# Mamba, attention, convolution and HGRN blocks on one core: shorter norm chains, attention's DVE and ACT steps on two blocks at a time, shuffled rotary partners

## The reference, cut to what matters

```python
# first two mixers:  h = rmsnorm(x, pre);  x = x + rmsnorm(mixer(h), post)
# the mamba mixer ends with:  y = rmsnorm(y, gate_norm);  return y @ w_out
def rmsnorm(x, w):
    return x * rsqrt(mean(x * x) + 1e-6) * w

# attention: 16 query heads, 4 key/value heads of 64, window 128, 4 blocks of 128 tokens
q, k = apply_partial_rope(q, cos, sin), apply_partial_rope(k, cos, sin)
# of each head's 64 rows, t1 = rows 0..7 and t2 = rows 8..15:
#   t1*cos - t2*sin,  t2*cos + t1*sin,  the rest as it is
s = (q . k) / 8, masked to the last 128 keys (256 key columns a block)
m = max(max(s), sink);  p = exp(s - m);  denom = sum(p) + exp(sink - m)
o = (p / denom) . v * silu(gate);  return o @ w_out
```

## Time and profile before

| what | us |
|---|---|
| three runs | 1970.71, 1975.97, 3117.33 (median 1975.97) |
| the profiled execution | 1969.06 |
| its span, first to last instruction | 1967.3 |
| PE busy / PEld busy in the span | 1872.2 / 1481.6 |
| DVE / ACT / POOL busy | 1078.4 / 611.2 / 905.7 |
| mean granted TensorE clock | 0.98 of full |

### The profile page before, as it was taken

How to read it: one execution, slowest core, us unless ns; L and a number is a source line. 1 busy time by engine, 2 the same in 40 slices (tenths; PEclk the granted TensorE clock), 3 DMA queues, 4 the chain that set the end, 5 groups by cost and what they waited for, 6 DMA issues and landing times.

```text
span 1967.3 us, 24972 instructions
## 1 busy us (share of the span) xinstructions
PE 1872.2 (95%) x9602; PEld 1481.6 (75%) x9602; DVE 1078.4 (55%) x1704; ACT 611.2 (31%) x1083; POOL 905.7 (46%) x910
## 2 busy tenths in 40 slices
PE   7999999897899897899999999999999999999997
PEld 5788877686676675558888888887777788888886
DVE  6888878834777756345333322148778753333212
ACT  5444445513333335023111100025566531111001
POOL 4444343354532245315555555554332455555552
PEclk9999999898999998999999999999999999999999
DMA  8676766576554454947889888896653498888884
GB/s 217 148 155 153 154 147 152 118 160 140 119 112 102 91 120 111 225 102 173 188 197 191 195 190 182 196 208 141 135 134 83 104 205 195 194 192 194 184 187 109
DMA packets 212838, 309.98 MB, mean 158 GB/s; under 512 B 22480, under 2 KB 166768, under 8 KB 212720
## 3 DMA queue, kind: packets, MB, share of 16 engines
q0 software_dynamic: 42624, 148.65, 44.2%
q1 hardware_dynamic: 165680, 154.34, 25.2%
q10 hardware_dynamic: 4416, 5.39, 1.1%
HBM read 153.18 MB, written 2.10 MB: 79 GB/s over the span
## 4 chain that ended last, share of the span: by engine, by line
PE 56%; DVE 1%; ACT 1%; ACTq 1%; DMA 1%; issue 1%; POOL 1%; DVEq 0%; POOLq 0%
PE gp L694 16%; PE gp L695 15%; PE gp L696 15%; PE mp L949 2%; PE mp L1025 1%; ACTq L1385 1%; PE gp L666 1%; PE gp L668 1%; PE gp L667 1%; PE gp L639 1%; PE gp L640 1%; PE gp L641 1%; PE mp L1075 0%; PE mp L1066 0%; POOL sqsum L564 0%
## 5 line engine op out<-in xcount | busy, mean ns | idle before, releaser
L584 POOL TENSOR_SCALAR wh<-stage 128x1024 fp32r<-128x1024 f32 (+2 forms) x298 | 344.1, 1155 | 906.0 <-PE gp L696 751.4
L694 PE MATMUL gp<-hh,wh 128*128 128x512 f32 x1512 | 607.4, 402 | 10.3 <-DVE m_raw L1661 4.3
L695 PE MATMUL gp<-hh,wl 128*128 128x512 f32 x1512 | 590.5, 391 | 0.0
L696 PE MATMUL gp<-hl,wh 128*128 128x512 f32 x1480 | 579.2, 391 | 0.0
L590 POOL TENSOR_SCALAR wl<-stage 128x1024 fp32r<-128x1024 f32 (+2 forms) x296 | 347.5, 1174 | 0.0
L694 PEld LDWEIGHTS gp<-hh,wh 128*128 128x128 f32 x1512 | 285.4, 189 | 77.3 <-issue 14.5
L695 PEld LDWEIGHTS gp<-hh,wl 128*128 128x128 f32 x1512 | 285.5, 189 | 58.5 <-issue 1.7
L696 PEld LDWEIGHTS gp<-hl,wh 128*128 128x128 f32 x1480 | 278.9, 188 | 59.9
L593 POOL DMA_DIRECT2D wl<-stage x296 | 261.9, 885 | 94.1 <-POOL wl L590 83.7
L2106 DVE TENSOR_TENSOR val<-gp,rstd 128x512 f32<-128x512 f32 x44 | 30.4, 691 | 203.9 <-PE gp L696 203.9
L694 PE MATMUL gp<-f_h,wh 128*128 128x512 f32 x352 | 137.2, 390 | 0.0
(11 more groups left out here) (352 smaller groups left out, 2805.7 us busy)
## 6 DMA issues: line engine op xcount, KB each, us to landing
wl<-stage POOLq DMA_DIRECT2D x263, 512.0 KB, 5.3
stage<-ffn_w SPq DMA_DIRECT2D x120, 512.0 KB, 4.2
stage<-ssm_w_in SPq DMA_DIRECT2D x32, 512.0 KB, 5.0
stage<-hg_w_in SPq DMA_DIRECT2D x32, 512.0 KB, 4.7
stage<-ssm_w_in SPq DMA_DIRECT2D x32, 256.0 KB, 5.0
stage<-ssm_w_out SPq DMA_DIRECT2D x16, 512.0 KB, 3.6
stage<-att_w_in SPq DMA_DIRECT2D x16, 512.0 KB, 4.7
stage<-cp_w_in SPq DMA_DIRECT2D x12, 512.0 KB, 5.4
```

The costliest lines, as they stand in the source:

```text
L584: pool.tensor_scalar(wh[:, s, part], stage[:, s, part], 1.0, 1.0, ALU.mult, ALU.mult).then_inc(hi_done, 1)
L694: pe.matmul(bank[:, :], wvh[:, cols], hi(kk), start=start, stop=False)
L695: pe.matmul(bank[:, :], wvl[:, cols], hi(kk), start=False, stop=False)
L696: mm = pe.matmul(bank[:, :], wvh[:, cols], lo(kk), start=False, stop=stop)
```

## The change

1. **Norm chains.** In both post-norms ACT squares the product straight out of PSUM, before DVE moves it to `yo` (a plain copy now). The gate norm's factor isn't applied: its epsilon is added to the sum of squares (`geps`), and Ln and Exp for `rg` go. In the two post-norms and the pre-norms of `att` and `cp` (`direct`) the eighth square isn't added; PE sums it by a second matmul. The table for Ln is loaded ahead of the last square.
2. **Pre-norms 0 to 2.** `val` goes; DVE forms the low part in one step, `xT*w - hh`. POOL's additions of squares go to DVE, between the residual steps. The sum stands in PE's program ahead of tile 7 of the lead units (`sum_early`).
3. **Tables** are made during `ssm_out`, after its fourth tile, with one more step (the sign of sin); ACT's Sin runs ahead of the last square.
4. **Rope.** The rotation matmuls go. DVE shuffles partner rows inside 32 partitions, then cos, sin and sum: four steps for three, at slots 4, 6 and 8. `turn_v` and `copy_v` have a semaphore of their own.
5. **Two blocks at a time.** `mask_scores`, `exps` and `normalise` handle two blocks of one head pair; the small steps are on 128x4. PE scores a pair in every second slot, ahead of `turn_p` and `pv`.
6. **Order.** A group's first slot has one granule and its second two (before: two and one). Setup of `kd`, the convolution's pads and `eye` moves ahead of the wait for `rstd`. `cp` runs 19 granules ahead of convolution 0 and 3 ahead of convolution 1 (before: 16 and 4).

```diff
     pre_round, post_round = [0, 2, 4, 5, 6, 7, 8], [1, 3]
+    direct = (1, 2, 3, 4)
+    own_eps = post_round[0]
...
-                for v, name in ((1, "att"), (2, "cp")):
-                    if u == phases[name][0] + 1:
-                        for k in range(1, KT):
-                            add_square(pool, pre_round[v], k)
...
             def sum_squares(r):
-                pe.wait_ge(sq_added, (KT - 1) * (r + 1))
-                pe.matmul(mp[3][:, :], ones[:, :], sqsum[:, :], start=True, stop=True).then_inc(sum_ready, 1)
+                pe.wait_ge(sq_added, adds_before(r + 1))
+                mm = pe.matmul(mp[3][:, :], ones[:, :], sqsum[:, :], start=True, stop=r not in direct)
+                if r in direct:
+                    pe.wait_ge(sq_ready, KT * (r + 1))
+                    mm = pe.matmul(mp[3][:, :], ones[:, :], sq[:, (KT - 1) % 2, :], start=False, stop=True)
+                mm.then_inc(sum_ready, 1)
...
                         if h < KVH:
                             late = h == KVH - 1
                             run(gran, ((1, 1, 1, 1, 1, 1, 1, 1, 0, 0, 0) if late else
-                                       (2, 1, 1, 1, 1, 1, 1, 1, 0, 1, 0))[k])
+                                       (1, 2, 1, 1, 1, 1, 1, 1, 0, 1, 0))[k])
...
                         if h:
+                            if k < 8 and k % 2 == 0:
+                                scores(h - 1, k // 2)
                             if 0 <= k - 2 < 8:
                                 turn_p(h - 1, k - 2)
                             if 0 <= k - 3 < 8:
                                 pv(h - 1, k - 3)
-                            if k < 8:
-                                scores(h - 1, k)
-                        if h < KVH and k == 9:
-                            rotate(h, (0, 1))
                     if h < KVH:
-                        rotate(h, (2,))
+                        turn_v(h)
...
-                run(gran, 16)
+                run(gran, 19)
                 convolve(0)
-                run(gran, 4)
+                run(gran, 3)
...
     # DVE, post_norm_of
+                    if k > 2:
+                        add_square(dve, pre_round[v], k - 2)
+                    if k:
+                        low_of_x(v, k - 1)
...
     # DVE, rope(h, j)
+                    shuffled = step(dve.stream_shuffle(rtmp[rows, 0, :], src, PARTNER))
+                    step(dve.tensor_tensor(rtmp[rows, 1, :], src, cosT[rows, :], ALU.mult))
+                    after(shuffled)
+                    step(dve.tensor_tensor(rtmp[rows, 0, :], rtmp[rows, 0, :], sinT[rows, :], ALU.mult))
+                    after()
+                    step(dve.tensor_tensor(dst, rtmp[rows, 0, :], rtmp[rows, 1, :], ALU.add))
...
     # DVE, the loop of attention
                         if h:
+                            if k == 6:
+                                gate_o(h - 1, 0)
                             if k == 11:
                                 gate_o(h - 1, 1)
-                            if 1 <= k <= 8:
-                                normalise(h - 1, k - 1)
-                            if k < 8:
-                                mask_scores(h - 1, k)
-                            if k == 6:
-                                gate_o(h - 1, 0)
+                            if k < 8 and k % 2:
+                                normalise(h - 1, k // 2)
+                            if k < 8 and k % 2 == 0:
+                                mask_scores(h - 1, k // 2)
...
-                            rope(h, (0, 1))
+                        if h < KVH and k in (4, 6, 8):
+                            rope(h, k // 2 - 2)
```

More of the change, by code:

```diff
@@ L238, in build, with adds_before @@
         n += count
+    unvalued = [split0[f"pre{v}"] for v in range(3)]
+    value0 = {name: n - KT * sum(u < n for u in unvalued) for name, n in split0.items()}
     y_split = [range(0, 4), range(4, 8), range(8, 10), range(10, 12), range(12, 13), range(13, 14)]
     pre_round, post_round = [0, 2, 4, 5, 6, 7, 8], [1, 3]
+    direct = (1, 2, 3, 4)
+    own_eps = post_round[0]
+    def adds_before(r):
+        return sum(KT - 1 - (i in direct) + (i == own_eps) for i in range(r))
     with ExitStack() as ctx:
@@ L618, in weights_at, with granules @@
                 return wh[:, s, at:at + un.cols], wl[:, s, at:at + un.cols]
-            def granules(name, hi, lo, split, lead=0, after_first=None, ahead=None):
+            def granules(name, hi, lo, split, lead=0, after_first=None, ahead=None, sum_early=False):
                 u0, u1, t0, _ = phases[name]
@@ L851, in mamba, with turn_v @@
                 run(gran_out)
-                pe.wait_ge(gate_rstd, 1)
+                pe.wait_ge(gate_eps, 1)
                 sum_squares(post_round[0])
             def attention():
[L856 to L870, removed]
+                gran = h_granules("att", "pre1", LEAD["att"], lambda: sum_squares(pre_round[1]), sum_early=True)
+                def turn_v(h):
+                    tile_taken(pe, tiles_of("att")[0] + 5 * h + 2)
                     if h:
@@ L875, in rotate, with scores @@
                     mm.then_inc(v_turned, 1)
-                def scores(h, i):
-                    t, n = i // 4, i % 4
+                def scores(h, q):
                     pe.wait_ge(qk_ready, h + 1)
[L880 to L887, removed]
+                    if h or q:
+                        pe.wait_ge(s_read, 4 * h + q)
+                    for b in range(2):
+                        t, n = q // 2, 2 * (q % 2) + b
+                        for j in range(2):
+                            k0 = max(n - 1, 0) * P
+                            w = (n + 1) * P - k0
+                            mm = pe.matmul(mp[b][:, (j + 1) * UC - w:(j + 1) * UC],
+                                           qr[:, h % 2, t, n * P:(n + 1) * P], kd[:, h % 2, j, k0:k0 + w],
+                                           start=True, stop=True)
                     mm.then_inc(s_ready, 1)
@@ L1640, in _, with tables @@
             dve.wait_ge(rstd_ready, pre_round[0] + 1)
+            def tables():
+                parts = two_pi_parts()
+                posf, t0, t1 = trig[0], trig[1], trig[2]
+                dve.wait_ge(posi_landed, 32)
+                step(dve.tensor_copy(posf[:, :], posi[:, :]))
+                after()
+                step(dve.tensor_scalar(posf[:, :], posf[:, :], cst[:, C_INV:C_INV + 1], None, ALU.mult))
+                after()
+                for dst, shift in ((sinT, 0.0), (cosT, 0.25)):
+                    step(dve.tensor_scalar(t0[:, :], posf[:, :], 0.15915494309189535, shift, ALU.mult, ALU.add))
+                    after()
+                    step(dve.tensor_scalar(t0[:, :], t0[:, :], MAGIC, None, ALU.add))
+                    after()
+                    step(dve.tensor_scalar(t0[:, :], t0[:, :], -MAGIC, None, ALU.add))
+                    after()
+                    src = posf
+                    for c in parts:
+                        step(dve.scalar_tensor_tensor(t1[:, :], t0[:, :], -c, src[:, :], ALU.mult, ALU.add))
+                        after()
+                        src = t1
+                    if shift:
+                        step(dve.tensor_scalar(t1[:, :], t1[:, :], float(np.pi / 2), None, ALU.add))
+                        after()
+                    ins = dve.tensor_scalar(dst[:, :], t1[:, :], PI_BELOW, -PI_BELOW, ALU.min, ALU.max)
+                    if shift:
+                        ins.then_inc(trig_ready, 1)
+                    else:
+                        step(ins)
+                        after()
+                        step(dve.tensor_scalar(dst[:, :], dst[:, :], cst[:, C_SIGN:C_SIGN + 1], None, ALU.mult))
             def mamba():
@@ L1888, in mask_scores, with normalise @@
+                    dve.tensor_tensor(four(8), sk, four(0), ALU.subtract).then_inc(m_ready, 1)
+                def normalise(h, q):
+                    s = q % 2
+                    dve.wait_ge(p_ready, 4 * h + q + 1)
+                    step(dve.tensor_tensor(srow[:, s, 12:16], srow[:, s, 12:16], srow[:, s, 16:20], ALU.add))
                     after()
-                    sk = sinks[:, HPG * h + 2 * (i // 4):HPG * h + 2 * (i // 4) + 2]
-                    step(dve.scalar_tensor_tensor(srow[:, b, 0:2], srow[:, b, 0:2], 0.125, sk, ALU.mult, ALU.max))
+                    step(dve.reciprocal(srow[:, s, 20:24], srow[:, s, 12:16]))
```

345 lines of the change are left out of this document (165 added, 180 removed).

## The result

The changed kernel takes 1948.14 us (median of four runs, 1946.3 to 1954.18). The ratio to the kernel before is 0.9884, 95% interval 0.9857 to 0.9910: some 23 us, 1.2%, gained. One of the four runs of the kernel before, 3117.33, is left out of the ratio as a slow one; the others took 1970.71, 1970.92 and 1975.97. The result lies in the forecast's wide range (1915 to 1958) and within 2%, but 1 us above the forecast's own range of 1930 to 1947. The forecast was 1937, so 11 us did not come. The profiled execution is the slowest of the four, 1954.18 (span 1952.4).

A forecast was written before the change was run, and what follows sets the result against it. PE's matmul pace was taken as fixed; its idle time and extra work between 470 and 863 could be saved. Gains 0.5 + 3.25 + 13 + 4 + 3.4 + 11 = 35.1 gave 1934 profiled, median 1937; own range 1930 to 1947, wide 1915 to 1958.

The forecast's parts named there:

- start: Pre-norm 0: ACT loses one step ahead of the first low part; gain between 0 and 1, taken as 0.5 us.
- post-norm 0: From the last product to `rstd`: 7.9 us now, 4.65 after; gain 3.25 us, with the tables hidden.
- `rstd` to first scores: Post-norm 0's `rstd` through pre-norm 1 and first rope: 54.0 us now, 41 after; gain 13 (10 to 16).
- groups: Attention groups of 46.5, 46.5 and 45.9 us, PE stalling 3.5 at each seventh block's turn; gain 4 (-6 to 14).
- post-norm 1: From the end of its products to `rstd`: 8.1 us now, 4.65 after; gain 3.4 us.
- `cp`: Lead units and convolution 0: no wait for shift DMAs, no half-speed start; gain 11 us (4 if DMAs end late).
- behind convolution 3: The later stages, given no term in the sum: expected as before, only earlier.
- The second rival: Attention stalls longer and clock falls: 2 us of POOL and 2.5 of clock on each of three stalls; 1951; chance 0.22.
- Everything behind 863 as before: A sign to look for: all work after 863 us in the profile unchanged, only earlier.

The follow-up runs named there:

- a3_same: The changed kernel again, unedited, run beside the others: 1946.69 us, ratio 0.9879 to the kernel before.
- f1_gates: c1_early with ACT's Silu of the gates moved: first gate from slot 7 to 9, last group's second from slot 2 to 8; 1917.99 us.
- d1_pool_late: The changed kernel with POOL's four weight halves in pre-norm 1's lead units held until the last low part stands: 1946.71 us.
- c1_early: The changed kernel with later pairs' scores ahead of their slot's granule, `gate_o` behind the mask and the second rope a slot later: 1926.79 us.
- b1_granule: The changed kernel with the granule of slot 9 moved to slot 8, ahead of the seventh block's turn, in the first two groups: 1943.4 us.
- b2_gate: The changed kernel with `gate_o` of the first head pair behind the mask in slot 6 instead of ahead of it: 1942.9 us.
- e1_cp16: The changed kernel with 16 and 4 granules of `cp` ahead of the first two convolutions instead of 19 and 3: 1948.78 us.
- a2_singles: The changed kernel with scores, mask, Exp and normalise on one block at a time, in the order of before: 1946.99 us.

## Why the prediction was in range, and 11 us short

Term by term, from the profiled executions:

| step | forecast | measured |
|---|---|---|
| start | 0.5 | 0 (2.5 in a3_same) |
| post-norm 0 | 3.25 | 3.6 |
| `rstd` to first scores | 13 | 8.7 |
| groups | 4 | -1.9 |
| post-norm 1 | 3.4 | 4.6 |
| `cp` | 11 | 8.9 |
| behind convolution 3 | 0 | -8.9 (-2.3 in a3_same) |

Up to convolution 3 that is 23.9 measured against some 35 forecast. The 11 us missing are 5.9 in the groups, 4.3 on the way to the first scores and 2.1 in `cp`, less the small terms. The start can't be told from single profiles: where the sum of post-norm 0 ends, behind almost the same code, lies between 469.3 and 473.4 in the eleven profiles of changed kernels.

- **Right.** `rstd` of post-norm 0 at 474.5 (forecast 474.8, which leaves out the sum's own 0.5), the first product at 477.75 (477.8), no wait for `wh`, the shuffle 0.74 (0.65 taken), tables hidden: DVE makes them from 428.6 to 444.9, and PE waits for nothing there. No wait at convolution 0, 7.07 long. Three of the seven terms came within 1.3 us.
- **Groups: the step that failed**, by its size and by a term put at nothing, the clock behind the wait. It said 46.5 for the first, as 43.0 of work and a wait of 3.5. The work is right: f1_gates shows 43.48 with hardly a wait. The wait is 4.34, with 0.85 of it POOL's (small steps of 0.60 and 0.57), and 3.0 us of low clock stand behind it, for which the sum had nothing. 43.5, 3.9 (the wait less the 0.41 that f1_gates has in its place) and 3.0 make the 50.4 measured. The second rival named just this mechanism, and the earlier trace rows already showed a turn of 1.09 behind a wait, so the sum had no reason to count its wait of 3.5 at its bare length. The rival's size is another matter: with 2 of POOL and 2.5 of clock on each of three stalls it took 13.5 off, while the groups fell 5.9 short (0.85 of POOL in the first, and 3.9, 2.4 and 0.8 in all against the three groups' forecast lengths). That its 1951 is 3 from the median is luck: the chain to the first scores and `cp` filled the gap.
- **Chain to the first scores**, mis-sized too. The last low part stands 24.4 behind `rstd`, not 22.6: POOL's hold is 4.3 (shown by d1_pool_late), 3 was taken. The wait of 3.86 which that makes inside the lead units was not foreseen, and eleven products behind it ran 0.43 apart instead of 0.23, some 2.2 us. Again a wait's clock.
- **`cp`**: 2.1 short, with convolution 0 at 60.9 instead of 58.6; no experiment splits that.
- **"Everything behind 863 as before" was wrong** in the first profile; the median hides it. Against the one profile of before, what eleven profiles gave back between convolution 3 and the last pre-norm lies between 0 and 8.9 us, mostly 1 to 4. That an unchanged stage, moved in time, has other DVE steps beside POOL's, and that this is the cause of the largest loss, was read from two traces, not tested.
- **Where the gain came from.** Norms 11, early tables 13, shuffles 0 to 3, pairs with their order 0. The part with most new code brought nothing in that order, since it relieved DVE, which had 12 us to spare in a group, and lengthened the chain from scores to turn. With the order of c1_early pairs go at 43.4 a group; whether single blocks would too was not tried.

The Trainium skill, SBUF — State Buffer, "Who interferes with whom", has the shared port as an exclusive lock, and d1_pool_late agrees in kind: the same three steps take 0.74, 0.68, 0.74 without POOL and 1.53, 1.52, 3.37 with it in a3_same. The Trainium skill, TensorE: Matmul & The Clock Gate, "HAM oscillation — how this bites in real kernels", says that a wait for DMA between two tiles makes the next tile start cold. The traces agree in part: the turns behind the waits of b1_granule and b2_gate take 1.09 and 1.12 instead of 0.60, while the 64 matmuls behind e1_cp16's wait of 2.59 ran at full clock.

## What to carry to other kernels

Price a wait of TensorE at its length and the low-clock stretch behind it, here up to 3 us behind waits of 1.93 to 4.34 among short matmuls, and none behind one of 2.59 before a convolution. Halving the wait brought 3 us in all, within the noise; removing it brought both. Before an engine off the path is relieved, look for the chain between one matmul and the next that needs its result, and issue its first step a granule earlier. With `gate_o` behind the mask and one rope a slot later, that brought 20 us here, where 6 us less of DVE's work in a group brought none. And time an unchanged stage behind the edit in more than one profile before its loss is put down to the edit.

## What the runs showed that was not expected

- A DVE step of 0.68 to 0.75 with two operands in SBUF took up to 3.37 beside two of POOL's conversions of 1.37; put off in time, the hold fell on one more step of rope (3.35 instead of 0.68).
- A wait of 2.59 before convolution 0 (e1_cp16) left its 64 matmuls at full clock, 7.07, while waits of 1.93 (b1_granule) and 1.89 (a2_singles) in the attention were followed by half speed. Before the change, 5.67 had given 9.79.
- The 512-element shuffle takes 0.74 and the next step starts 0.63 behind it; the load of its mask, 0.01.
